# Expert layer of a two-block transformer step: the row-fetched block's top-k first, all its dot products in the first expert stage, bf16 one-hots and gate parts, and every fourth low half of the second stage on GpSimd

## The reference

```python
q = (xb @ wq).reshape(PEER_BLOCK, PEER_HEADS, 2, PEER_HALF)          # 8 heads, 2 halves of 128
s = jnp.einsum('thpd,hpkd->thpk', q, sub_keys)                       # 128 keys per half
s_top, i_top = lax.top_k(s, PEER_TOPK)                               # 16 of 128
cand_s = s_top[:, :, 0, :, None] + s_top[:, :, 1, None, :]           # 256 candidates per head
best_s, best_pos = lax.top_k(cand_s, PEER_TOPK)                      # 16 of 256
experts = jnp.take_along_axis(cand_i, best_pos, axis=-1)             # i * 128 + j
g = jax.nn.softmax(best_s, axis=-1)
act = jax.nn.gelu(jnp.einsum('thkd,td->thk', expert_u[experts], xb))
return jnp.einsum('thk,thkd->td', g * act, expert_v[experts])        # 8 * 16 experts per token
```

## Time and profile before

| | us |
|---|---|
| median of 3 runs | 2530.11 |
| lowest and highest run | 2529.14, 2533.96 |
| span of the profiled execution | 2531.0 |
| TensorE busy | 2427.7 (96%) |
| VectorE busy | 1535.4 (61%) |
| ScalarE busy | 939.2 (37%) |
| GpSimd busy | 1213.8 (48%) |

### The profile page before, as it was taken

The page is one execution under the profiler, slowest core; times in us unless marked ns, Lnnn a source line. Parts: engine busy times, 40 slices in busy tenths (PEclk is TensorE's granted clock), DMA queues, the critical chain, the costliest instruction groups (busy, mean ns, idle before and its releaser), DMA issues.

```text
span 2531.0 us, 37403 instructions
## 1 busy us (share of the span) xinstructions
PE 2427.7 (96%) x12832; PEld 2161.3 (85%) x12832; DVE 1535.4 (61%) x2699; ACT 939.2 (37%) x1412; POOL 1213.8 (48%) x676
## 2 busy tenths in 40 slices
PE   7999998999999999978899989999999999999998
PEld 4878887899999999978888889998867888888887
DVE  5268343079979996769999999887246414422201
ACT  4463333244445554322333334333344323322222
POOL 3214443446678885555555554334411544444443
PEclk9999999999999999999999999999999999999999
DMA  7238333335555758999999999993311333223332
GB/s 278 67 121 294 134 98 93 99 116 176 176 161 198 267 208 308 362 354 399 399 399 399 400 400 380 360 342 112 94 41 42 113 95 100 89 94 99 96 96 75
DMA packets 254203, 514.53 MB, mean 203 GB/s; under 512 B 117728, under 2 KB 150880, under 8 KB 250016
## 3 DMA queue, kind: packets, MB, share of 16 engines
q1 hardware_dynamic: 197264, 345.82, 40.9%
q0 software_dynamic: 38416, 142.36, 14.2%
q10 hardware_dynamic: 18432, 25.17, 2.7%
HBM read 460.85 MB, written 52.43 MB: 203 GB/s over the span
## 4 chain that ended last, share of the span: by engine, by line
PE 65%; DVE 13%; DMA 8%; SPq 8%; issue 3%; ACT 1%; POOL 0%; DVEq 0%; ACTq 0%; POOLq 0%
PE bank L1240 16%; PE bank L1241 16%; PE bank L1242 16%; DMA GJ<-gate_dram 4%; PE pair L1240 4%; PE pair L1241 4%; PE pair L1242 4%; SPq L499 3%; DMA T<-in_u_rows,which 3%; SPq L582 2%; SPq L583 2%; PE pair L1563 2%; DVE T L2252 1%; DVE T L2129 1%; DVE T L2167 1%
## 5 line engine op out<-in xcount | busy, mean ns | idle before, releaser
L621 POOL TENSOR_TENSOR wlo<-wraw,whi 128x1024 fp32r<-128x1024 f32 x303 | 746.9, 2468 | 847.0 <-ACT whi L745 843.7
L1240 PE MATMUL bank<-HH,whi 128*128 128x512 f32 (+1 forms) x2048 | 747.3, 365 | 26.2 <-ACT actb L946 7.1
L1241 PE MATMUL bank<-HL,whi 128*128 128x512 f32 (+1 forms) x2048 | 742.5, 363 | 0.0
L1242 PE MATMUL bank<-HH,wlo 128*128 128x512 f32 (+1 forms) x2048 | 742.2, 362 | 0.0
L745 ACT ACTIVATE whi<-wraw 128x1024 fp32r<-128x1024 f32 x456 | 481.4, 1057 | 570.4 <-PE bank L1242 214.9
L1240 PEld LDWEIGHTS bank<-HH,whi 128*128 128x128 f32 x2048 | 385.7, 188 | 76.3 <-issue 24.1
L1242 PEld LDWEIGHTS bank<-HH,wlo 128*128 128x128 f32 x2048 | 385.5, 188 | 40.3
L1241 PEld LDWEIGHTS bank<-HL,whi 128*128 128x128 f32 x2048 | 385.7, 188 | 39.8 <-issue 0.5
L701 POOL DMA_INDIRECT VROW<-in_w,which x128 | 213.1, 1665 | 203.8 <-DVE YROW L2310 198.4
L1240 PE MATMUL bank<-WH,whi 128*128 128x384 f32 x512 | 181.0, 353 | 42.9 <-DVE WL L2287 42.9
L694 POOL DMA_INDIRECT T<-in_u_rows,which x128 | 145.5, 1137 | 158.1 <-DVE dots L2252 151.2
(11 more groups left out here) (411 smaller groups left out, 3650.7 us busy)
## 6 DMA issues: line engine op xcount, KB each, us to landing
wraw<-in_w SPq DMA_DIRECT2D x456, 512.0 KB
act_dram<-actb ACTq DMA_DIRECT2D x128, 192.0 KB
gate_dram<-GS SPq DMA_DIRECT2D x24, 1024.0 KB, 10.1
AJ<-act_dram SPq DMA_DIRECT2D x128, 192.0 KB
GJ<-gate_dram SPq DMA_DIRECT2D x128, 192.0 KB
adaw<-in_ada SPq DMA_DIRECT2D x32, 512.0 KB
ada<-in_ada SPq DMA_DIRECT2D x16, 512.0 KB, 13.9
NB<-in_nab POOLq DMA_DIRECT2D x4, 1024.0 KB
```

The lines of the kernel that those rows point to most:

```text
L621: nc.gpsimd.tensor_tensor(wlo[:, slot, :, :].rearrange("p k c -> p (k c)"), wraw[:, slot, :, :].rearrange("p k c -> p (k c)"), whi[:, slot ...
L1240: pe.matmul(out_, ah, bh, start=first, stop=False, **kw)
L1241: pe.matmul(out_, ah, bl, start=False, stop=False, **kw)
L1242: return pe.matmul(out_, al, bh, start=False, stop=last, **kw)
```

## The change

It has five parts.

1. **Order.** `ORDER = (3, 0, 1, 2)`: the block whose experts are fetched row by row has its top-k first. The lead before the gates is 64 tiles instead of 48 (`LEAD_IT = 16`), the tail behind the gates 12 instead of 28.
2. **Dots early.** The row buffer moves to `X`, which is saved to DRAM ahead (2 MB) and reloaded in the V stage. 12 dots stand in each of the last three top-ks, 72 among the 96 gate groups, 20 behind them. None is left in V.
3. **Gates in bf16.** One-hots of i and j come from one `tensor_tensor` of 1024 elements, `indices_hot`, with both inputs in SBUF; the gates, split into three bf16 parts, are multiplied in by another of 1536 elements, `gates_hot`, again with both in SBUF. A group is 12 matmuls of 128x128 in bf16. VectorE's sum L2224, `window` and GpSimd's `OJ` go.
4. **GpSimd.** It makes all low halves of U (before: those up to the end of the gates), and issues the fetches of rows between them by a fixed schedule. The last 16 rows are issued behind the low half of tile 127.
5. **V stage.** The low half of each fourth tile is GpSimd's, between its fetches (`v_lo`); the other three stay VectorE's.

```diff
+STEPS = SD // 4
+LEAD_IT = 16
+GATE_IT = LEAD_IT + 1
+U_GATE = STEPS // 8
 U_TAIL = 32 - GATE_IT - U_GATE
+ORDER = (TD, *range(TD))
+DOTS_TOP, DOTS_GATE = 12, 72
+FETCH_AT = 16
...
-        UROW = T[:, :, :].rearrange("p a b -> p (a b)").rearrange("p (n c) -> p n c", c=D)
+        UROW = X[:, :, :].rearrange("p a b -> p (a b)").rearrange("p (n c) -> p n c", c=D)
...
+            sp.wait_ge(tile_evac, G0["wq"])
+            sp.dma_start(x_dram[:, :, :], X[:, :, :]).then_inc(x_saved, 16)
...
             pool.wait_ge(rows_known, 1)
-            pool.wait_ge(og_ready, 32 * TD)
-            for k in range(LEAD + R):
+            pool.wait_ge(x_saved, 16)
+            pool.wait_ge(n_scaled, 3 * KB)
+            for k in range(R):
+                fetch_u(k)
+            fetched = R
+            gate0 = 4 * GATE_IT + 3
+            for t in range(FETCH_AT, P):
+                lo(G0["U"] + t, t % R)
+                if t < gate0:
+                    due = R + min((t - FETCH_AT) * 3 * DOTS_TOP // (4 * LEAD_IT - FETCH_AT), 3 * DOTS_TOP)
+                else:
+                    due = R + 3 * DOTS_TOP + min(t + 1 - gate0, 4 * U_GATE) * DOTS_GATE // (4 * U_GATE)
+                for k in range(fetched, min(due, P)):
+                    fetch_u(k)
+                fetched = max(fetched, min(due, P))
+            for k in range(fetched, P):
                 fetch_u(k)
...
+            for k in range(P):
                 fetch_v(k)
+                if k % 4 == 2:
+                    pool.wait_ge(w_hi, G0["V"] + k + 2)
+                    nc.gpsimd.tensor_tensor(wlo[:, 3, :, :].rearrange("p k c -> p (k c)"),
+                                            wraw[:, 3, :, :].rearrange("p k c -> p (k c)"),
+                                            whi[:, 3, :, :].rearrange("p k c -> p (k c)").bitcast(F32),
+                                            ALU.subtract).then_inc(v_lo, 1)
...
                 for e in range(4):
-                    t = 4 * half + e
-                    mm = pe.matmul(bank[4 + 2 * half + e // 2][:, e % 2 * 256:e % 2 * 256 + 256], OI[:, t, :],
-                                   OG[:, half, :, e, :], start=True, stop=True)
+                    for part in range(3):
+                        mm = pe.matmul(bank[4 + slot][:, e * P:(e + 1) * P], OH[:, slot, 0, :, e],
+                                       OG[:, slot % 2, part, :, e], start=(part == 0), stop=(part == 2))
                 mm.then_inc(g_done, 1)
...
+                def settled(ins, between=True):
+
+                    ins.then_inc(dve, 1)
+                    chain.add()
+                    turns[0] += between
+                    if n and between and turns[0] <= DOTS_TOP:
+                        dot()
+                    v.wait_ge(dve, chain.at())
...
+            def indices_hot(q):
+
+                if q >= 4:
+                    v.wait_ge(g_done, q - 3)
+                nc.vector.tensor_tensor(OH[:, q % 4, :, :, :], bc(iota4[:, :, :], 1, 2), bc(IJ[:, q, :, :], 2, P),
+                                        ALU.is_equal).then_inc(oh_ready, 1)
+
+            def gates_hot(q):
+
+                v.wait_ge(oh_ready, q + 1)
+                if q >= 2:
                     v.wait_ge(g_done, q - 1)
...
+                nc.vector.tensor_tensor(OG[:, q % 2, :, :, :], bc(OH[:, q % 4, 1, :, :], 1, 3), bc(G3[:, q, :, :], 2, P),
+                                        ALU.mult).then_inc(og_ready, 1)
+
+            indices_hot(0)
+            for q in range(STEPS):
+                if q + 1 < STEPS:
+                    indices_hot(q + 1)
+                gates_hot(q)
+                if (q + 1) * DOTS_GATE // STEPS > q * DOTS_GATE // STEPS:
+                    dot()
...
+            while dotted[0] < P:
+                dot()
```

More of the change, by code:

```diff
@@ L667, in _ @@
             pool.dma_start(keysT, A["keys"]).then_inc(keys_in, 16)
[L668 to L680, removed]
-                    offsets_j(i * 32 + n, n % 4, peeled=(first and n < 4))
-                    if n % 2:
-                        lo(i * 16 + (gu0 + 3 + n // 2), (n // 2 + 3) % R)
-            pool.wait_ge(j_rows, 1)
-            gate_blocks(0, True)
-            with pool.Fori(1, TD) as i:
-                gate_blocks(i, False)
+            los(G0["wq"] + 3, G0["U"] + FETCH_AT - G0["wq"] - 3)
             def fetch_u(k):
@@ L1025, in v_tiles @@
                     pw_tile(i * 4 + (u + 3), (u + 3) % R)
[L1027 to L1040 removed]
+            ahead(G0["V"] + 124, 0)
+            pw_tile(127, 127 % R)
             ahead(G0["V"] + 124, 1)
@@ L2146, in topk @@
                                         bc(two[:, :, 0:8], 2, 7), ALU.add)
-                then(nc.vector.tensor_tensor(best[:, :, 72:80], one[:, :, 8:16], bc(two[:, :, 0], 2, 8), ALU.add))
+                settled(nc.vector.tensor_tensor(best[:, :, 72:80], one[:, :, 8:16], bc(two[:, :, 0], 2, 8), ALU.add), False)
                 sixteen(lambda h: best[:, h, :], lambda h: bv[:, h, :], lambda h: bp[:, h, :], NH)
@@ new lines, in _ @@
+            for n in range(1, TB):
+                topk(n)
+            v.wait_ge(tk_exp, TB)
+            by_head = gsel[:, :, :].rearrange("p t (h k) -> p (t h) k", h=NH)
+            then(nc.vector.tensor_reduce(hs[:, 0, :], by_head, AX_X, ALU.add))
+            then(nc.vector.reciprocal(hs[:, 1, :], hs[:, 0, :]))
+            nc.vector.tensor_tensor(by_head, by_head, bc(hs[:, 1, :], 2, 16), ALU.mult).then_inc(tk_gate, 1)
+            v.wait_ge(gt_turned, 1)
+            nc.vector.tensor_copy(iota4[:, :, :], bc(iota[:, :], 2, 4))
@@ L2246, in lo @@
                                         ALU.subtract).then_inc(w_lo, 1)
-            def dot(n, u, turns):
-                v.wait_ge(u_row[u], turns)
-                column = dots[:, n:n + 1]
-                nc.vector.tensor_tensor_reduce(UROW[:, u, :], UROW[:, u, :], sc_row, 1.0, 0.0, ALU.mult, ALU.add, column)\
-                    .then_inc(dot_done, 1)
             def expert_weights(i):
@@ L2320, in v_steps @@
                     v_step(i * 4 + u, u, i)
[L2321 to L2332 removed]
+            v.wait_ge(dot_act, 1)
+            v_steps(0)
+            with v.Fori(1, 31) as i:
+                v_steps(i)
             expert_weights(31)
```

286 lines of the change are left out of this document (118 added, 168 removed).

## The result

The changed kernel takes 2630.7 us in the median (2626.7 to 2631.8, four runs), the kernel before 2532.0 (2529.1 to 2536.5, four runs) beside it: ratio 1.038, interval 1.0364 to 1.0397, so it is slower by 3.8%. The profiled execution has a span of 2624.9 us, 93.9 more than before. The medians lie 98.7 us apart; the profiled execution is the fastest of its four, and what stands behind V took anything from 804.5 to 811.2 us in the profiled executions of this document, though no edit touches it. Slower was forecast, 2573 us was not, nor did the range reach so far (2498 to 2625).

The account below looks back on a forecast made before the run. TensorE was taken as the bound nearly everywhere before, VectorE and GpSimd in turn in the new gates. Terms: +110.6 us before V, -68 in V, together +42.6 on the profiled 2531.0, so 2573 us; range 2498 to 2625.

Parts of the forecast that it names:

- the price of a dot in the lead: Lead top-ks: each dot costs 1.8 us, including 0.65 us waiting for GpSimd's low halves; 65 us for 36 dots.
- the 798 of the sum: Lead: the last top-k ends near 569.7 + 151 + 65 + 12 = 798 us.
- TensorE's wait in the lead: Lead: TensorE, through 64 tiles at 787.5 us, waits about 11 us for the last top-k, between 0 and 20.
- 3.44 us per group: Gate stage: VectorE and GpSimd in turn set the pace, 1.48 + 0.86 + 1.10 us per group; 330 us in all.
- the likeliest case: Whole kernel: gates at 3.44 us per group, chance 0.55, with its own range from 2545 to 2605 us.
- Boundary: Gates into V: late rows in four turns of 10.2 us, last dot near 1225 us, V starts near 1233.
- the sign: End of U: a gap of over 30 us on TensorE ahead of tile 127 would show the forecast right.
- V: V stage: without dots it runs at TensorE's floor, 533 + 2 us, a gain of 68 us.
- That bf16 doesn't wait for GpSimd: Gates: TensorE's 2.77 us per group sets the pace, gates 266 us, kernel faster at 2501 us; chance 0.23.
- That the two-byte forms run at the f32 rate: Gates: 4.78 us per group, 459 us for the stage, kernel at 2702 us; chance 0.08.
- That V stays above its floor: V: GpSimd's low half delays the next V row; 4.5 us per tile, V 576 us, kernel 2616; chance 0.10.

Follow-up runs that it names:

- the gap between them: Changed kernel with each of GpSimd's unrolled U low halves waiting until the one before has ended: 2617.1 us, ratio 1.0315.
- the dot with PSUM: Changed kernel with the dot's second operand read from two PSUM banks instead of its SBUF copy: 2574.1 us, ratio 1.0152.
- the repairs: Changed kernel plus, stacked: dot operand from PSUM, gate operands in pairs, all dots early, gate low halves on VectorE: 2497.7 us, ratio 0.9855.
- two schedules together: Changed kernel with lead fetches four tiles later and each GpSimd low half waiting for the previous one's end: 2604.3 us, ratio 1.0265.

## Why the prediction was off

**What failed: the price of a dot in the lead.** The step was "a dot meets one with a chance near 0.58 and then waits 1.1 us on average: 0.65 us". Measured: 2.93 - 1.21 = 1.72 us per dot, over 36 dots 62 us instead of 23. The chance was right: 21 of 36 dots were held up, 0.58. The wait was wrong: 2.95 us for each of the 21, not 1.1. Half of one low half's 2.2 us is what a dot pays that arrives at any moment of a single one. Here the low halves stood in step with the dots, so that a dot that met one low half waited 1.97 us on average, and one that met two or three in a row 4.04. That the row of low halves matters is shown by the gap between them: the wait per meeting fell to 1.38 us, with 25 meetings. That all of it comes from the second SBUF input is shown by the dot with PSUM: nothing is left. Why two low halves were due so often is shown less well. In the trace they fall due while GpSimd waits in a fetch for a dot, but with 60% of this waiting gone it still happened 12 times instead of 15; the schedule itself has a low half without a fetch behind it in every fourth tile.

**Other terms of the lead.** VectorE's last top-k chose its columns by 840.9 us, 42.9 later than the 798 of the sum. The dots make 38 of it. The one-hot steps, taken at their old price, rose from 2.82 to 4.48 us, 10 us in all, and a step on 64 elements (L2178) from 0.22 to 2.69, 7 us; other steps came out shorter. TensorE's slower matmuls (0.183 us) cost little: it stood at the transposes 15.9 us before VectorE was done, and the four tiles behind took 18.0 us instead of 16.8. The step bounded TensorE's wait in the lead at 0 to 20 us; at its end it was 15.9, but the sum had no stop for a low half that GpSimd made late, and with those it was 43.2. The lead had no dear end, and so the range had none either.

**Gates, right in size, wrong in the engine.** 3.44 us per group was forecast for VectorE and GpSimd in turn; the run with the moving operand side by side gives 3.47. TensorE was bounded at 2.77 to 3.45 us and came out at 3.53: the 0.114 us of the earlier trace rows was taken for the dear end, and 0.118 lay beyond it. That row is of the same shape in f32 with its elements side by side; it says nothing of a step of 8 bytes. The stage took 339.3 us, 96 groups at 3.53, where the sum had 326. The sums also had slips: 96 x 3.44 less two groups is 323, not 326, and the low end of the likeliest case (3.2 us per group, no wait in the lead) adds up to 2539, not 2545. That the total came so near is partly luck, since two limits of nearly the same height stood behind each other.

**Boundary, right in kind.** The rows come in turns of four through GpSimd's queue, and all of V stands behind the last dot. Tile 127 waited 27 us; over 30 was named as the sign. From tile 116 to V it took 80.0 us against 89 forecast, because a turn of four rows took 7.5 us and not 10.2 (from the first dot at 1245.4 us to the 13th at 1268.0). Dealing all but one of these rows to earlier stages removes the stop and gives 26 us.

**V, right.** From V's first matmul to its last 538.2 us, before 603.1 by the same measure (first matmul at 1122.42, last at 1725.53): -64.9 against -68. The rest is the low halves given to GpSimd, taken as free: without them V takes 534.2 us. The gain is kept in each version above; in the changed kernel V starts 159.5 us later for it.

**The rivals.** That bf16 doesn't wait for GpSimd: refuted by the 3.00 us beside 0.68. That the two-byte forms run at the f32 rate: refuted by 0.68 and 0.95. That V stays above its floor: refuted by 533.1 us for 3057 matmuls. The page SBUF — State Buffer of the Trainium skill, "Who interferes with whom", says that with at most one SBUF input, outside its two-port modes, VectorE doesn't contend with GpSimd; the trace agrees, 1.21 us for all dots read from PSUM. It also puts a tensor_tensor with two SBUF inputs among those that do; the trace agrees for bf16, 3.00 us. On the same page, "SBUF cachelines", two accesses to a 16-byte line are enough for the full rate; an 8-byte step has two, and the runs show 0.118 us against 0.057 at a 4-byte step. Here the measurement decides.

**Where the time went.** By the medians the repairs give 56.6 us for the lead, 31.9 for the gates' matmul step, 26.3 for the late rows and 18.2 for GpSimd's turns in the gates, 133 in all.

## What to carry to other kernels

When an instruction can wait for another engine's, the number of meetings is the easy half; ask what one meeting costs. Half of the other instruction's length is right only for a chance arrival at a single one. If the other engine waits for yours in between, it can start in step with you, and what fell due meanwhile can stand in a row: the sum needs a dear end at the full length of one or two for every meeting. Here 21 meetings were forecast and 21 came, at 2.95 us and not 1.1. Before scheduling around such a conflict, look for an operand that already lies in PSUM: one edit there was worth 56 us, two schedules together 25 to 26. And a repaired bound shows its worth only once the bound behind it is gone (6 us alone, 32 after the first repair).

## What the runs showed of the hardware that was not expected

- A bf16 matmul of 128 columns with a load each starts every 0.118 us with a moving operand at 8-byte steps, every 0.057 at 4-byte steps and every 0.056 side by side; taking the 8-byte steps from the stationary operand alone changes it by 0.002 us.
- Two of GpSimd's low halves issued back to back keep VectorE out for both: one instruction of 1.21 us took 5.42. With the second issued only after the first had ended, the longest of 36 took 3.8.
- A dot whose second operand is read from PSUM takes 1.21 us beside GpSimd's low halves, as it does alone, while those take 2.50 us in the mean.
- A wait costs TensorE more than its length: 24 matmuls behind a stop of 27 us took 6.8 us instead of 4.16 (mean granted clock 0.58), and a lead of 275 us with 43 us of stops ran its matmuls 6% slower (0.92).
